# One queue order, fewer stores and another hand-over in the sampled attention of a two-layer decoder step

## The reference

```
z = einsum('bqhd,bkhd->bhqk', q * d**-0.5, k) + bias
log_1mb = log_sigmoid(-z)
excl = reverse cumulative sum of log_1mb, without the own key
att = exp(log_sigmoid(z) + excl)
out = einsum('bhqk,bkhd->bqhd', att, v)
```

## Time and profile before

| | us |
|---|---|
| median of 3 runs (3162.14 to 3166.29) | 3164.81 |
| the profiled execution | 3165.45 |
| its span, first to last instruction | 3163.7 |
| PE busy | 2913.2 |
| DVE busy | 2101.6 |
| ACT busy | 1291.1 |
| POOL busy | 724.9 |

### The profile page before, as it was taken

One profiled execution on the slowest core, in us unless ns is written; L12 is line 12 of the kernel. 1 busy time (PEld: TensorE's weight loads), 2 busy tenths in 40 slices (PEclk: granted clock), 3 DMA queues, 4 the chain that ended last, 5 costly groups with the idle time before them and its releaser, 6 DMA issues. The chain is left out here.

```text
span 3163.7 us, 70060 instructions
## 1 busy us (share of the span) xinstructions
PE 2913.2 (92%) x27683; PEld 2367.9 (75%) x27683; DVE 2101.6 (66%) x3283; ACT 1291.1 (41%) x2293; POOL 724.9 (23%) x697
## 2 busy tenths in 40 slices
PE   8999999978898988998899999989989999998898
PEld 7899999967776766776887777877756666667676
DVE  9526666647666647885487677604639888887576
ACT  2225555434444435342310100012228888875332
POOL 5000000012232211110011111101227666664111
PEclk9999999989999989999999999999989999999999
DMA  6624545454443556552789999865450101008342
GB/s 214 204 95 151 154 151 153 140 162 117 105 116 87 130 150 195 158 174 84 260 253 342 319 330 322 294 192 170 149 193 6 68 14 55 15 20 257 124 158 77
DMA packets 470335, 502.83 MB, mean 159 GB/s; under 512 B 200065, under 2 KB 362866, under 8 KB 464986
## 3 DMA queue, kind: packets, MB, share of 16 engines
q1 hardware_dynamic: 373466, 339.83, 35.8%
q10 hardware_dynamic: 88032, 142.51, 13.0%
q0 software_dynamic: 8512, 16.02, 1.7%
HBM read 357.13 MB, written 141.31 MB: 158 GB/s over the span
## 5 line engine op out<-in xcount | busy, mean ns | idle before, releaser
L3029 POOL TENSOR_TENSOR sp_att<-sp_beta,sp_left 128x512 f32<-128x512 f32 (+3 forms) x320 | 302.3, 955 | 187.0 <-DVE sp_left L2990 172.6
L120 PE MATMUL po_acc<-po_x_high,po_w_low 128*128 128x412 f32 (+1 forms) x840 | 306.6, 365 | 15.1 <-DVE po_x_low L113 13.7
L120 PE MATMUL pe_acc<-pe_x_high,pe_w_low 128*128 128x412 f32 (+1 forms) x840 | 302.6, 360 | 5.4 <-PEq L86 5.4
L121 PE MATMUL po_acc<-po_x_low,po_w_high 128*128 128x412 f32 (+1 forms) x840 | 299.5, 357 | 0.0
L122 PE MATMUL po_acc<-po_x_high,po_w_high 128*128 128x412 f32 (+1 forms) x840 | 298.7, 356 | 0.0
L121 PE MATMUL pe_acc<-pe_x_low,pe_w_high 128*128 128x412 f32 (+1 forms) x840 | 293.7, 350 | 0.0
L122 PE MATMUL pe_acc<-pe_x_high,pe_w_high 128*128 128x412 f32 (+1 forms) x840 | 293.3, 349 | 0.0
L2990 DVE TENSOR_TENSOR_SCAN sp_left<-sp_z,sp_left,sp_zero 128x512 f32<-128x512 f32 x192 | 235.7, 1269 | 18.3 <-ACT sp_z L2951 14.0
L2654 DVE TENSOR_TENSOR po_work<-po_work,po_q 128x1024 f32<-128x1024 f32 x128 | 177.6, 1388 | 83.3 <-DMA po_work<-in_cache_k 74.4
L2943 ACT ACTIVATE sp_beta<-sp_z,sp_bias 128x512 f32<-128x512 f32 (+3 forms) x320 | 183.1, 628 | 94.1 <-PE sp_z L2881 47.7
L1371 ACT COPY po_o<-po_acc 128x412 f32<-128x412 f32 (+1 forms) x105 | 52.5, 500 | 392.2 <-PE po_acc L122 337.2
(11 more groups left out here) (492 smaller groups left out, 6979.8 us busy)
## 6 DMA issues: line engine op xcount, KB each, us to landing
po_work<-in_cache_k SPq DMA_DIRECT2D x256, 256.0 KB, 4.8
po_work<-in_cache_v ACTq DMA_DIRECT2D x256, 256.0 KB, 4.6
scratch_ops<-pe_work SPq DMA_DIRECT2D x160, 128.0 KB, 2.0
out_z<-pe_o SPq DMA_DIRECT2D x84, 206.0 KB, 2.8
out_z<-po_o ACTq DMA_DIRECT2D x84, 206.0 KB, 4.2
pe_w<-in_w_e SPq DMA_DIRECT2D x21, 512.0 KB, 6.0
rc_opx<-scratch_ops SPq DMA_DIRECT2D x64, 160.0 KB, 3.7
po_w<-in_w_o ACTq DMA_DIRECT2D x20, 512.0 KB
```

The source lines that it names most:

```text
L120: pe.matmul(out, ll, rh, start=start, stop=False)
L121: pe.matmul(out, lh, rl, start=False, stop=False)
L3029: pool.tensor_tensor(att[h][:, n % 3, 0:w], be[h][:, n % 4, 0:w], left[h][tile(n) % 2][:, at + 1:at + 1 + w], ALU.mult).then_inc(at_ok[h], 1)
```

## The change

Three edits, all around `po`.

First, DVE's list in a slot: the chain's steps come ahead of the slot's `scores`.

```
             for t in range(START, TAIL):
                 if t in chain:
                     bias_on(chain[t])
-                for p in at(pairs, t):
-                    scores(p)
                 if t - 1 in chain:
                     clamp(chain[t - 1])
                 if t - 2 in chain:
                     softplus(chain[t - 2])
                 if t - 3 in chain:
                     argument(chain[t - 3])
                 if t - PER - 3 in chain:
                     diagonal(chain[t - PER - 3])
+                for p in at(pairs, t):
+                    scores(p)
```

```
-        self.ot = s.sb("o", [P, self.PIECES, BLK])
+        self.ot = s.sb("o", [P, self.PIECES, BLK] if self.pinned else [P, COLS])
...
+    def runs(self):
+        row, latest = [], {}
+        for t, (i, n, b) in enumerate(self.slot):
+            self.run_past[t] = latest.get(b)
+            row.append(b)
+            after = self.slot[t + 1] if t + 1 < self.slots else None
+            if after == (i, n, b + 1) and row != [0, 1]:
+                continue
+            count = self.run_count[row[0]] = self.run_count.get(row[0], 0) + 1
+            for x in row:
+                latest[x] = row[0], count
+            self.run_end[t] = row[0], b
+            row = []
+
+    def store_run(self, eng, t):
+        if t in self.run_end:
+            first, last = self.run_end[t]
+            lo, hi = first * BLK, min(COLS, (last + 1) * BLK)
+            eng.wait_ge(self.evicted, t + 1)
+            eng.dma_start(self.out[self.slot[t][1], :, lo:hi], self.ot[:, lo:hi]).then_inc(self.kept[first], 16)
...
+    def evict_run(self, copy, eng, t, more=()):
+        lo, hi = self.columns(t)
+        bank = self.acc[t % self.banks]
+        if self.run_past[t]:
+            first, count = self.run_past[t]
+            eng.wait_ge(self.kept[first], 16 * count)
+        eng.wait_ge(self.done, t + 1)
+        for dst in more:
+            copy(dst, bank[:, hi - lo - NS:hi - lo])
+        copy(self.ot[:, lo:hi], bank[:, 0:hi - lo]).then_inc(self.evicted, 1)
...
-                    pj.evict(act.copy, act, t, more)
-                    pj.store(act, t)
+                    pj.evict_run(act.copy, act, t, more)
+                    pj.store_run(act, t)
...
-            for t in range(pj.slots - pj.PIECES, pj.slots):
-                pj.stored(act, t)
+            pj.runs_stored(act)
```

```
             sp.wait_ge(out, 1)
-            sp.dma_start(cat[0:4, :, SEQ:COLS].rearrange("n p c -> p n c"), oc[:, :, :]).then_inc(stored, 16)
-            sp.wait_ge(stored, 16)
+            sp.dma_start(cat[0:4, :, SEQ:COLS].rearrange("n p c -> p n c"), oc[:, :, :]).then_inc(values_ahead.cat_put, 16)
...
                               gc[:, :, :].rearrange("p n b -> p (n b)"), ALU.mult).then_inc(out, 1)
+            values_ahead.split_x(dve)
...
-    FRONT = 4
+    FRONT = 2
...
         for k in range(self.FRONT):
             self.weights(sp, k)
-        self.tile(sp, 1)
...
             for k in range(ahead.FRONT, KT):
                 ahead.weights(sp, k)
+            ahead.tile(sp, 1)
...
             sp.wait_ge(late, 48)
+            sp.wait_ge(ahead.cat_put, 16)
...
-            ahead.split_x(dve)
             for k in range(KT):
                 ahead.low_w(dve, k)
```

More of the change, by code:

```diff
@@ L1265, in __init__ @@
         self.done, self.evicted = s.sem("done"), s.sem("evicted")
-        self.kept = [s.sem(f"kept{n}") for n in range(self.PIECES)]
+        self.kept = [s.sem(f"kept{n}") for n in range(self.PIECES if pinned else NBLK)]
         self.slot = [(i, n, b) for i, (n, blocks) in enumerate(groups) for b in blocks]
@@ L1271, in __init__ @@
             self.begin.setdefault(i, t)
+        self.run_end, self.run_past, self.run_count = {}, {}, {}
+        if not pinned:
+            self.runs()
         self.opens = {t: i for i, t in self.begin.items()}
@@ L1283, in place, with runs_stored @@
             self.wh, self.wl = s.sb("w_high", [P, 2, KT * P]), s.sb("w_low", [P, 2, KT * P])
-        self.ot = s.sb("o", [P, self.PIECES, BLK])
+        self.ot = s.sb("o", [P, self.PIECES, BLK] if self.pinned else [P, COLS])
         self.acc = [s.ps(f"acc{n}", [P, 512]) for n in range(self.banks)]
+    def runs(self):
[17 more added lines that the diff above has]
+            eng.dma_start(self.out[self.slot[t][1], :, lo:hi], self.ot[:, lo:hi]).then_inc(self.kept[first], 16)
+    def runs_stored(self, eng):
+        for first, count in self.run_count.items():
+            eng.wait_ge(self.kept[first], 16 * count)
[4 more added lines that the diff above has]
+            first, count = self.run_past[t]
+            eng.wait_ge(self.kept[first], 16 * count)
+        eng.wait_ge(self.done, t + 1)
+        for dst in more:
+            copy(dst, bank[:, hi - lo - NS:hi - lo])
+        copy(self.ot[:, lo:hi], bank[:, 0:hi - lo]).then_inc(self.evicted, 1)
     def columns(self, t):
@@ L2472, in project_odd @@
         (cst, tab, q_tr, q_ev, q_st, set_, prod, k_used, v_used, biased, exp_, cl, ln, spl, tri_pe, own_, arg, att_ok,
-         o_ev, o_pe, gate, out, stored) = (s.sem(n) for n in (
+         o_ev, o_pe, gate, out) = (s.sem(n) for n in (
              "cst", "tab", "q_tr", "q_ev", "q_st", "set", "prod", "k_used", "v_used", "biased", "exp", "cl", "ln",
-             "sp", "tri_pe", "own", "arg", "att", "o_ev", "o_pe", "gate", "out", "stored"))
+             "sp", "tri_pe", "own", "arg", "att", "o_ev", "o_pe", "gate", "out"))
         k_in, v_in = [s.sem(f"k_in{n}") for n in range(KR)], [s.sem(f"v_in{n}") for n in range(VR)]
@@ L2731, in __init__ @@
         self.w_low, self.x_in = [s.sem("w_low_even"), s.sem("w_low_odd")], [s.sem("x_in0"), s.sem("x_in1")]
-        self.x_high, self.x_low = s.sem("x_high"), s.sem("x_low")
+        self.x_high, self.x_low, self.cat_put = s.sem("x_high"), s.sem("x_low"), s.sem("cat_put")
     def tile(self, sp, t):
```

3 lines of the change are left out of this document (1 added, 2 removed).

## The result

The changed kernel takes 3122.2 us (median of 4 runs, 3119.6 to 3127.1), the kernel before 3163.5 in the same comparison: ratio 0.987, interval 0.9853 to 0.9887.

A forecast was written before the change was run, and what follows sets the result against it. It took PE to bound `po`, with the DMAs close behind and ACT's late issuing causing PE's waits. Terms 8.0 + 4.9 + 8.0 - 0.5 + 2.7 + 2.9 - 2.0 = 24.0 us gave 3141 us, range 3128 to 3159.

The forecast's parts named there:

- po_att: In `po`, seven samples: `po_att` comes 0.7 us earlier, gaining 4.9 of 14.7 us of PE's waits; ends 2.5 to 6.3.
- I take 0.7: ACT's time saved per chain slot without a store and its wait for the copy, in us; between 0.36 and 0.9.
- Clock: In `po`: shorter idling before `po_att` avoids half-clock stretches, gaining 8.0 of 12.4 us; ends 0 and 12.4.
- I count two thirds: Share of the 12.4 us lost to half clock in six samples of `po` expected back: 8.0 us.
- Maximum of samples 2 to 8: In `po`: ln comes 1.1 us earlier, so PE's wait of 9.0 us falls to about 1, gaining 8.0.
- First sample: In `po`: DVE's new order lets PE go on 2.7 us sooner after the maximum, or 4.6 if POOL does not block it.
- Seam: From `po` to `pv`: barrier 2.6 us sooner, PE 0.9 sooner still, 0.6 given back; net 2.9 us, bounds 0 and 4.
- Pages: In `po`: nearly full DMAs make value pages land later, costing 2 us more of PE's waits; ends 0 and 8.
- Rival 1: The DMAs cap `po`: a sample's period stays above 57.7 us plus gaps, say 59.9, giving 3149 us; chance 0.17.
- Start: Slots 5 to 7 of `po`: copies wait for stores to land, delaying queries and first chain 0 to 3 us; 0.5 taken.
- Rival 2: ACT gains nothing in `po`, page loads being held by something else; only 5.6 us gained, 3159 us; chance 0.09.
- rival 3: DVE becomes the bound in `po`, standing at the clamp while no keys flow; slower, 3172 us; chance 0.05.

The follow-up runs named there:

- self_wait: The changed kernel, but ACT waits for its own copy in the slots without a store too; ratio to the kernel before 0.9879.
- order_only: The kernel before with one edit: DVE takes the chain's step ahead of the slot's scores; ratio 0.9983.
- stores_only: The kernel before with one edit: the stores issued by runs of blocks; ratio 0.9893.
- no_order: The changed kernel with DVE's order of before; ratio to the kernel before 0.9863.
- late_store: The kernel before with the stores of the slots of exp, ln and `po_att` moved behind the activation, none removed; ratio 0.9886.
- act_first_before: The kernel before with ACT's activation of the chain ahead of the slot's page loads, stores and DVE's order as before; ratio 0.988.
- act_first: The changed kernel with ACT's activation of the chain ahead of the slot's page loads; ratio to the kernel before 0.986.

## Why the prediction fell short

The direction, the late engine and the order of the causes were right: ACT's issuing, not DVE's order, held samples 2 to 8. The result left the range because `po_att` and the clock went past even their upper ends (6.3 and 12.4), by 2.9 and 1.9 us, first sample and seam went 0.4 and 0.7 past theirs, and nothing was lost to pages. Term by term:

- *`po_att`, 4.9 us forecast, 9.2 measured.* The step that failed is "I take 0.7" per slot. The store and the wait are 1.05 together (0.5 + 0.55, by self_wait), because the weight load of that slot runs beside the copy too. The mean wait fell by 1.3: the other 0.3 is the slot's first load of a page number, which took 0.28 to 1.09 us in the seven slots before and 0.28 or 0.29 after; why is open.
- *Clock, 8.0 forecast, 14.3 measured.* "I count two thirds" failed: all six of the counted stretches went. They cost 13.7 us and not 12.4 (half of PE's busy time in them); the first sample's, 1.6, which the prediction left out, went too, and a new one of 1.7 came behind the second sample's maximum. With waits of 0.8 instead of the 1.1 to 1.4 that I expected all of samples 2 to 8 kept the clock at `po_att`. So the first term's error brought this one with it.
- *Maximum of samples 2 to 8, 8.0 forecast, 5.1 measured.* No wait was left in six samples, as forecast, but the working does not give that. A shift of 1.1 us, taken from waits of 0.56 to 1.79, makes 6.6 and not 8.0 (and 0.36 us a slot makes a shift of 0.7, not the 1.1 behind "still 6.5"); in the third sample a maximum of 1.20 us would have ended near 1755.9. The rest came from what the prediction had not reckoned with: in samples 3, 4, 5 and 8 of the kernel before the maximum ran beside POOL's cast and took 0.99 to 1.20 us, in the changed kernel those take 0.43. So six samples were right in part by luck. What failed is that DVE is free in time everywhere: in the second sample two pairs went ahead of the maximum, the second of them after a wait of 2.3 us for its keys, and it met POOL, a wait of 3.9 us.
- *First sample, 2.7 forecast, 5.0 measured, plus the clock.* I had the maximum blocked by POOL's low part for 2.3 us. It began 119.1 us after po's first matmul, where I had 121.9, and took 1.00, beside POOL's cast. The step that failed is that this gain is DVE's order's: order_only keeps 4.6 of the 6.5 us (there the maximum did meet POOL's low part, and took 2.42), while stores_only and no_order wait 1.5 and 1.6 us with the old order. (The clamp's row, which the prediction calls agreeing, could not tell what the maximum pays, since the clamp reads one tile and the maximum two; the maximum's own rows above do.) There and in the changed kernel the first scores began 58 to 59 us into `po` (before: 62.7). But order_only began them at 58.9 too and late_store at 62.2, so how much of this is the freer start of the copies and how much scatter is open.
- *Seam, 2.9 forecast (3.5 at once, 0.6 given back), 4.7 measured at once.* Tile 0 landed sooner than 6.6 us:

```profile
2083.75 0.55 SPq L2774 DMA_DIRECT2D pv_x<-scratch_x1T  x1
...
2090.02 0.69 DVE L108 CAST pv_x_high<-pv_x 128x1024 fp32r<-128x1024 f32 x1 [3.29 <-DMA pv_x<-scratch_x1T]
2090.75 1.23 DVE L113 TENSOR_TENSOR pv_x_low<-pv_x,pv_x_high 128x1024 fp32r<-128x1024 f32 x1
```

  6.3 us from issue to split, 0.3 less than reckoned; the other 0.8 is that PE starts 3.6 us behind the split's end and not 4.4 (5.3 - 0.9). The edit's own gain was 6.0; "only the pieces are larger; I cost this at nothing" failed here, since with the stores' edit 1.4 of that was lost. Of the 4.7 `pv` gives some more back: its first 168 matmuls take 41.0 us instead of 39.9 in this pair, 41.0 to 41.8 in the ten kernels with the new passage and 39.9 to 41.0 in the six with the old one, 0.7 by the means.
- *Pages, -2.0 forecast, +1.9 measured.* The share rose to 0.96 and 339 GB/s, and PE waited for no page. Rival 1 fell: its floor of 57.7 us of DMA time a sample was none. After the change the values behind `po_att` start at 1697.0 in the second sample and 2038.6 in the eighth, 56.9 us a sample, which at a share of 0.96 is 54.7 us of DMA time for nearly the same bytes. The Trainium skill's rule beside it (DMA: Bandwidth & Descriptors, "Issuing engines are not separate DMA queues"), that the issuing engines share the same DMA engines and only time of issuing is saved, was taken to speak for 3149. It did not: here the time of issuing was itself on the path, and act_first_before shows 39 us from it without a byte changed.
- *Start, -0.5 forecast, +1.4 measured.* The waits between the single blocks show as no wait of PE; the 1.4 are scatter, as said above, and not a gain.

Rival 2 fell by late_store, rival 3 by act_first: with PE's waits for `po_att` gone altogether DVE still kept up.

## What to carry to other kernels

Where an engine both issues transfers and computes a step that others wait for, count its queue from the step's release to the step, instruction by instruction, issues and self-waits included; then put the step first and the issues behind it. Moving three issues behind the step gave 33 us here, removing them 33 by the totals and 39 by po's length. And price an idle PE with the clock behind it: a wait shortened until the dips stayed away gave back more than itself (9.2 us of waits for `po_att`, some 14 of clock). Look at what a larger transfer shortly ahead of a barrier may cost: the stores by runs lost 1.4 to 1.6 us there.

## What the runs showed of the hardware

- A weight load's DMA issue starts 0.02 us after a copy on ACT has begun (1748.95 and 1748.93), and the first page's DMA 0.70 us after, with the load of the page number ahead of it: ACT's issues run beside its own copy unless a semaphore holds them.
- DVE's 128x256 maximum takes 0.41 to 0.43 us alone. Two that began while POOL's cast or low part was under way ended 0.28 and 0.27 us behind POOL's instruction: 1.00 us in the changed kernel's first sample (1625.18, the cast ended at 1624.90), 2.50 in its second (1683.29 and 1683.02). The four slow ones of the kernel before (0.99 to 1.20 us, samples 3, 4, 5 and 8) did the same behind the cast. One that began just ahead of POOL's cast kept its 0.42 us, and the cast took 1.26 us instead of 1.04 (kernel before, second sample).
- The stage `rc`, the same code in all 16 kernels and far ahead of the change, took from 521.2 to 529.4 us between its first matmul and the next stage's, in one profile of each. Totals of a few us apart say nothing about an edit here; the length of the stage itself leaves this scatter out, but not its own.
